# Attention blocks turned in pairs, with their high-half products moved behind their own turns

## The chip, the cores and the metric

One core of a Trainium2 chip runs the whole kernel in one launch. The metric is the time of one execution on the device, in microseconds; the kernel before was run three times (1393.4 to 1393.8 us, median 1393.6).

## The reference

One layer of a decoder on 1024 tokens of width 1024: RMSNorm and one wide input projection; two mixers beside each other, a sparse attention and a causal pooling; each is multiplied by a sigmoid gate (1024 channels each), added, projected and added to the residual; then RMSNorm, an MLP with squared ReLU (4096 wide), and a last RMSNorm. The attention has 8 heads of 64 in two groups of four, and three branches that each have a softmax of their own:

```
s_c = q k_cmp  - slope * dist        63 compressed keys
s_s = q k_slc  - slope * dist        all earlier keys (the 16 best of 16 blocks of 64)
s_w = q k_win  - slope * dist        the last 512 keys
o   = g0 * softmax(s_c) v_cmp + g1 * softmax(s_s) v_slc + g2 * softmax(s_w) v_win
```

Everything is float32.

## The kernel before, in words

Float32 products are made of rounded halves: x = hi + lo, and a product is three matmuls, `ahi*whi`, `alo*whi`, `ahi*wlo` (lines 2248 to 2250 in the helper `three`), each 128x512. The program is written out for each engine, with semaphores by hand; nothing is scheduled by a tool.

The attention stage, the one that is changed, has 16 iterations `it`, eight for each group of four heads, in the order of query tiles 7, 1, 6, 2, 5, 3, 4, 0 (`ITER`). A tile i has i+1 blocks of 128 keys of the selected branch (`slc`), up to five of the window (`win`), and one of the compressed keys (`cmp`, always last): 14, 5, 13, 7, 12, 9, 11 and 3 blocks. Block numbers B run on over all iterations. An iteration has four quarters r; `chunk(it, r)` is the list of blocks of a quarter, a quarter of the iteration's blocks, rounded.

For one block:

- `turn` (TensorE, line 2517): four 128x128 transposes, one per head, from the probabilities `prob` into bank B % 2 of `psX`. It waits for `pt_lo` of block B-2 (the bank is free).
- `prob_hi` (ACT, line 1215): rounds the bank to `pth[B % 2]`, 128x512. It waits for the turn and for the high product of B-2.
- `prob_lo` (DVE, line 1868): what the rounding left, to `ptl[B % 2]`. It waits for `prob_hi` and for the low product of B-2.
- `high_product` (TensorE, line 2532, `pth` times the values, waits `pt_hi`) and `low_product` (line 2538, `ptl`, waits `pt_lo`). Both add into bank 2 of `psX`. The `cmp` block has one product, of line 2545, which with the last low product forms `last_products`, at the end of the iteration or, in front of even iterations, a little into the next.

At the head of each quarter TensorE makes the scores of the next iteration for head r (lines 2495 to 2508). DVE adds the masks and takes the maxima (lines 1823, 1834, 1838) and makes the bias `nb` (line 1842); ACT takes three exponentials for them (line 1207, one per branch, the first waits for `nb`); DVE divides (lines 1854, 1856) and raises `p_ready`.

ACT has one queue in program order. In a quarter it holds: `prob_hi` of the first block, exponential 1, `prob_hi` of the second, exponential 2, and so on; in the first quarter of even iterations two `prob_hi` stand in front of exponential 1. This order is the same before and after.

In the first 14 iterations (`Z_STEPS`) the gate products of the mixers are spread between the block work: 16 steps per iteration, four per quarter, each step one k of a 1024-deep product, that is three matmuls (`gates(q, lo, hi)`, written into bank 2 or 3 of `psX`). `GATE_LEAD` puts two of the four steps of the first quarter of even iterations ahead of the first turn. `share` cuts what is left of a quarter's steps into 2 parts per block. The order within a quarter of n blocks was, for each block: its turn, the low product of the block two back, a part of the gate steps, the high product of the block one back, another part.

Of the kernel before, what the change touches and what calls it, by code (L numbers as in the profile page):

```python
# [16 lines left out]
def hybrid_trunk(nc, x, norm1_g, w_in, cmp_pe, cmp_w1, cmp_w2, w_attn_proj, w_pool, pool_scale,  # L17
# [75 lines left out]
    with ctx:  # L93
# [14 lines left out]
        def place(name, shape, dt=f32):  # L108
            off = cursor[0]
            cursor[0] += size_of(shape)  # L110
            assert cursor[0] <= END, (name, cursor[0] - END)
            return nc.alloc_sbuf_tensor_at(name, shape, dt, offset=off)
# [10 lines left out]
        gates = place("gates", [P, TT, HEADS, 3])  # L123
# [285 lines left out]
        def chunk(it, r):  # L409

            b = blocks(ITER[it][1])
            lo, hi = [round(len(b) * c / GR) for c in (r, r + 1)]
            return [(first_block[it] + k, *b[k]) for k in range(lo, hi)]
# [9 lines left out]
        Z_STEPS = 2 * KT - 2  # L423
# [3 lines left out]
        def gate_share(it, r):  # L427

            if it < Z_STEPS:
                return it + 1, KT // 2 * r, KT // 2 * (r + 1)  # L430
            c, n = (2 * r, 2) if it == Z_STEPS else (2 * GR + r, 1)
            return Z_STEPS + 1, c, c + n
# [6 lines left out]
        def prob_col(i, kind, kb):  # L439
            if kind == "slc":  # L440
                return kb * P
            if kind == "win":
                return n_slc(i) + (kb - (i + 1 - n_win(i) // P)) * P
            return n_slc(i) + n_win(i)
# [3 lines left out]
        def gate_bank(q, h):  # L448

            return psX[:, 2 if q == 0 and h == 1 else 3]  # L450
# [124 lines left out]
        block = ctx.enter_context(nc.Block())  # L575
# [1669 lines left out]
        def _(pe):  # L2245
            def three(ps, slot, k, w, hi, lo, cols, start, stop):

                nc.tensor.matmul(ps, whi[:, slot, w], hi[:, k, cols], start=start, stop=False)  # L2248
                nc.tensor.matmul(ps, whi[:, slot, w], lo[:, k, cols], start=False, stop=False)  # L2249
                return nc.tensor.matmul(ps, wlo[:, slot, w], hi[:, k, cols], start=False, stop=stop)  # L2250
# [233 lines left out]
            def scores(it, r):  # L2484
                g, i = ITER[it]
                e = it * GR + r
                s = it % 2
                if r == 0:
                    pe.wait_ge(q_lo, it + 1)
                if e >= 1:  # L2490
                    pe.wait_ge(m_slc, e)
                a, w = n_slc(i), n_win(i)
                for c in range(0, a, HALF):
                    n = min(HALF, a - c)
                    nc.tensor.matmul(psS0[:, c:c + n], qh[:, s, r], kS[:, g, c:c + n], start=True, stop=False)
                    last = nc.tensor.matmul(psS0[:, c:c + n], ql[:, s, r], kS[:, g, c:c + n], start=False, stop=True)  # L2496
                last.then_inc(s_slc, 1)
                if e >= 1:
                    pe.wait_ge(m_win, e)
                nt = w // P  # L2500
                whole = nt if nt == HALF // P else nt - 1
                if whole:
                    out, ks = psS1[:, 0:whole * P], kW[:, g, i + 1 - nt:i + 1 - nt + whole, 0:P]
                    nc.tensor.matmul(out, qh[:, s, r], ks, start=True, stop=False)
                    nc.tensor.matmul(out, ql[:, s, r], ks, start=False, stop=True)
                out, ks = psS1[:, whole * P:w + CP], kW[:, g, i, (whole - nt + 1) * P:WC]
                nc.tensor.matmul(out, qh[:, s, r], ks, start=True, stop=False)
                nc.tensor.matmul(out, ql[:, s, r], ks, start=False, stop=True).then_inc(s_win, 1)

            def turn(it, B, kind, kb):  # L2510

                g, i = ITER[it]
                if B >= 2:
                    pe.wait_ge(pt_lo, B - 1)
                col = prob_col(i, kind, kb)
                for r in range(GR):
                    last = nc.tensor.transpose(psX[:, B % 2, r * P:(r + 1) * P], PB[it % 2][:, r, col:col + P], ident[:])  # L2517
                last.then_inc(t_done, 1)

            def stacked(it, kind, kb):  # L2520

                return {"slc": vS, "win": vW}[kind][:, kb, ITER[it][0]]

            def high_product(it, B, kind, kb):

                if B == first_block[it]:
                    if it:
                        pe.wait_ge(o_ready, it)
                    else:
                        pe.wait_ge(z_ready, 2)  # L2530
                pe.wait_ge(pt_hi, B + 1)
                nc.tensor.matmul(psX[:, 2], stacked(it, kind, kb), pth[:, B % 2], start=B == first_block[it],
                                 stop=False).then_inc(high_done, 1)

            def low_product(it, B, kind, kb):

                pe.wait_ge(pt_lo, B + 1)
                nc.tensor.matmul(psX[:, 2], stacked(it, kind, kb), ptl[:, B % 2], start=False, stop=False).then_inc(low_done, 1)

            def last_products(it):  # L2540

                B = first_block[it + 1] - 1
                low_product(it, B - 1, *blocks(ITER[it][1])[-2])
                pe.wait_ge(pt_lo, B + 1)
                nc.tensor.matmul(psX[:, 2], vC[:, ITER[it][0]], pth[:, B % 2], start=False, stop=True).then_inc(high_done, 1)

            def gates(q, lo, hi):

                n, slot = NZ + q, (NZ + q) % 2
                for h, k in [divmod(c, KT) for c in range(lo, hi)]:  # L2550
                    if h == 0 and k == 0:
                        pe.wait_ge(w_lo, n + 1)
                    if k == 0 and q:
                        pe.wait_ge(z_ready, 2 * q + h if q > 1 or h else 1)
                    last = three(gate_bank(q, h), slot, k, k, ahi, alo, slice(h * HALF, (h + 1) * HALF), k == 0, k == KT - 1)
                    if k == KT - 1:
                        last.then_inc(u_done, 1)
# [8 lines left out]
                scores(0, r)  # L2566
                gates(0, lo, hi)
            for it in range(NIT):
                recent = []
                for r in range(GR):  # L2570
                    if it + 1 < NIT:
                        scores(it + 1, r)
                    if r == 0 and it and GATE_LEAD[it]:
                        last_products(it - 1)
                    todo = chunk(it, r)
                    q, g0, g1 = gate_share(it, r)
                    if it == r == 0 or not todo:
                        lead = g1 - g0
                    else:
                        lead = GATE_LEAD[it] if r == 0 else 0  # L2580
                    share = [g0 + lead + (g1 - g0 - lead) * k // max(1, 2 * len(todo)) for k in range(2 * len(todo) + 1)]
                    gates(q, g0, g0 + lead)
                    if r == 0:
                        pe.wait_ge(p_ready, GR * (it + 1))
                    for k, (B, kind, kb) in enumerate(todo):
                        turn(it, B, kind, kb)
                        if len(recent) > 1:
                            low_product(it, *recent[-2])
                        gates(q, share[2 * k], share[2 * k + 1])
                        if recent:  # L2590
                            high_product(it, *recent[-1])
                        recent.append((B, kind, kb))
                        gates(q, share[2 * k + 1], share[2 * k + 2])
                if it + 1 == NIT or not GATE_LEAD[it + 1]:
                    last_products(it)
            gates(2 * KT - 1, KT + GR, 2 * KT)
# [282 lines left out]
```

## Time and profile before

| | |
|---|---|
| median of 3 runs | 1393.6 us |
| the profiled execution: device time | 1393.44 us |
| the profiled execution: span | 1391.7 us |
| TensorE busy in it | 1377.7 us |
| DVE, ACT, POOL busy | 1034.5, 736.8, 198.6 us |
| granted TensorE clock | 0.998 |
| attention stage (scores of iteration 0 to the last block product) | 190.8 to 571.3 us |
| in it: turns | 148 blocks, 592 transposes |

In a timeline row the first number is the start in us from the span's start, the second the length of what is merged into the row, then engine, line, operation, tiles, shapes, and how many instructions; in brackets the idle time of the engine before it and what ended it. PE is the matmul side of TensorE, PEld its weight loads. The records of matmuls overlap, since they are pipelined: the distance of two starts is what a matmul takes of the engine's time, not the record's length.

### The profile page before, as it was taken

What the parts mean: (1) busy time and instruction counts of PE and PEld (TensorE: products, weight loads), DVE (VectorE), ACT (ScalarE), POOL (GpSimd) and SP (SyncE); (2) the same over time, 40 slices, a digit from 0 to 9 for tenths busy, and PEclk for the clock granted to TensorE, in tenths of its full rate; (3) what the DMA queues carried; (4) which work ended last, traced back from release to release, by engine and by line L of the source; (5) the groups of instructions that cost most, each with busy time, mean ns of one, the idle gap of its engine ahead of it and who ended that gap; (6) DMA issues with size and microseconds to landing.
All of it is one profiled execution on the core that took longest, in us unless ns stands there. A gap on an engine that the chain in (4) does not pass through costs nothing.

```text
span 1391.7 us, 19091 instructions
## 1 busy us (share of the span) xinstructions
PE 1377.7 (99%) x6589; PEld 1140.6 (82%) x6589; DVE 1034.5 (74%) x2040; ACT 736.8 (53%) x1427; POOL 198.6 (14%) x199
## 2 busy tenths in 40 slices
PE   9999999999999999999999999999999999999997
PEld 7788788888888888788888888888888888888886
DVE  7986577888788888866568877778695968777664
ACT  6433246666666666622235655545454646555554
POOL 5132000101010100000230030211213030302100
PEclk9999999999999999999999999999999999999999
DMA  6446531222221121654222174654639191836553
GB/s 222 129 144 179 153 92 57 65 61 58 62 72 57 47 65 54 219 184 162 77 91 91 47 143 100 127 109 88 132 81 161 53 165 56 155 88 133 94 167 121
DMA packets 162109, 151.75 MB, mean 109 GB/s; under 512 B 12659, under 2 KB 125095, under 8 KB 162016
## 3 DMA queue, kind: packets, MB, share of 16 engines
q1 hardware_dynamic: 145888, 121.20, 28.7%
q0 software_dynamic: 16128, 29.37, 14.4%
q8 instruction: 51, 0.84, 0.2%
q14 instruction: 42, 0.34, 0.1%
HBM read 94.43 MB, written 56.10 MB: 108 GB/s over the span
## 4 chain that ended last, share of the span: by engine, by line
PE 95%; DVE 3%; ACT 1%; issue 1%; DVEq 0%; POOL 0%; POOLq 0%; ACTq 0%
PE psU L2248 5%; PE psU L2249 5%; PE psU L2250 5%; PE psX L2517 5%; PE psU L2695 4%; PE psU L2697 4%; PE psX L2248 4%; PE psU L2696 4%; PE psX L2249 4%; PE psX L2250 4%; PE psU L2732 4%; PE psU L2734 4%; PE psU L2733 4%; PE psX L2695 3%; PE psX L2697 3%; PE psX L2696 3%
## 5 line engine op out<-in xcount | busy, mean ns | idle before, releaser
L1024 POOL DMA_DIRECT2D residual_scratch<-csum x112 | 98.2, 911 | 482.1 <-DVE csum L2147 414.4
L1970 DVE TENSOR_TENSOR ring_lo<-raw,ring_hi 128x512 fp32r<-128x512 f32 x150 | 103.1, 687 | 64.9 <-ACT ring_hi L1327 64.9
L1327 ACT ACTIVATE ring_hi<-raw 128x512 fp32r<-128x512 f32 x150 | 92.8, 626 | 63.8 <-PE psU L2734 22.8
L1215 ACT ACTIVATE pth<-psX 128x512 fp32r<-128x512 f32 x148 | 87.4, 596 | 71.2 <-PE psX L2517 71.0
L1868 DVE TENSOR_TENSOR ptl<-psX,pth 128x512 fp32r<-128x512 f32 x132 | 90.4, 688 | 29.4 <-ACT pth L1215 28.7
L1207 ACT ACTIVATE prob<-prob,nb 128x640 f32<-128x640 f32 (+7 forms) x128 | 93.8, 733 | 31.9 <-DVE nb L1842 31.7
L2248 PE MATMUL psX<-ahi,whi 128*128 128x512 f32 x256 | 102.8, 401 | 0.1
L2249 PE MATMUL psX<-alo,whi 128*128 128x512 f32 x256 | 100.8, 394 | 0.0
L2250 PE MATMUL psX<-ahi,wlo 128*128 128x512 f32 x256 | 100.4, 392 | 0.0
L2517 PE MATMUL psX<-ident,prob 128*128 128x128 f32 x592 | 88.4, 274 | 1.4 <-DVE prob L1856 0.6
L2248 PE MATMUL psU<-ahi,whi 128*128 128x512 f32 x216 | 84.7, 392 | 0.0
L996 POOL TENSOR_TENSOR wlo<-wraw,whi 128x1024 fp32r<-128x1024 f32 x14 | 33.6, 2401 | 357.1 <-DVE prob L1856 357.1
L2249 PE MATMUL psU<-alo,whi 128*128 128x512 f32 x216 | 84.1, 389 | 0.0
L2250 PE MATMUL psU<-ahi,wlo 128*128 128x512 f32 x216 | 84.1, 389 | 0.0
L2517 PEld LDWEIGHTS psX<-ident,prob 128*128 128x128 f32 x592 | 68.5, 140 | 16.1 <-DVE ptl L1868 4.2
L1402 ACT ACTIVATE csum<-psU 128x512 f32<-128x512 f32 x84 | 49.5, 598 | 39.2 <-PE psU L2734 31.0
L1408 ACT ACTIVATE csum<-csum 128x512 f32<-128x512 f32 x64 | 40.5, 633 | 49.8 <-DVE csum L2104 49.8
L1823 DVE CUSTOM_DVE_ANT_0 prob<-psU,T 128x1024 f32<-128x1024 f32 (+7 forms) x64 | 48.1, 752 | 24.4 <-PE psU L2496 24.3
L1970 DVE TENSOR_TENSOR ring_lo<-t,ring_hi 128x512 fp32r<-128x512 f32 x60 | 41.2, 686 | 32.3 <-ACT ring_hi L1327 32.3
L1854 DVE TENSOR_SCALAR prob<-prob,rs 128x640 f32<-128x640 f32 (+7 forms) x128 | 57.5, 492 | 2.3
L2250 PEld LDWEIGHTS psX<-ahi,wlo 128*128 128x128 f32 x256 | 48.1, 188 | 11.1
L1327 ACT ACTIVATE ring_hi<-t 128x512 fp32r<-128x512 f32 x60 | 37.8, 630 | 35.7 <-DVE t L1983 23.6
(374 smaller groups left out, 3989.0 us busy)
## 6 DMA issues: line engine op xcount, KB each, us to landing
raw<-in_w_ff_dram SPq DMA_DIRECT2D x120, 256.0 KB, 4.4
residual_scratch<-csum POOLq DMA_DIRECT2D x112, 256.0 KB, 5.9
wraw<-in_w_in_dram SPq DMA_DIRECT2D x23, 512.0 KB, 4.1
gate_scratch<-zst SPq DMA_DIRECT2D x32, 256.0 KB, 2.8
mg<-gate_scratch SPq DMA_DIRECT2D x16, 512.0 KB, 3.4
proj_scratch<-stage SPq DMA_DIRECT2D x30, 256.0 KB, 2.2
xt<-in_x_dram SPq DMA_DIRECT2D x8, 512.0 KB, 6.9
duo_w<-in_w_in_dram SPq DMA_DIRECT2D x16, 256.0 KB, 4.2
```

The lines of the kernel that those rows point to most:

```text
L1024: pool.dma_start(resid[rows, cols], sums[b][e][:], accum_op=ALU.add).then_inc(added[b][e], 16)
L1207: nc.scalar.activation(cols, cols, ACT.Exp, scale=2.0 ** -(g * GR + r + 1), bias=nb[:, it % 2, r, b:b + 1], accum_out=esum[:, it % 2, r, b ...
L1327: nc.scalar.activation(weights_of(g)[0], raw_of(g), ACT.Copy).then_inc(w_hi, 1)
L1868: nc.vector.tensor_tensor(dst[part, B % 2], psX[part, B % 2], pth[part, B % 2].bitcast(f32), ALU.subtract).then_inc(pt_lo, 1)
L1970: nc.vector.tensor_tensor(lo, raw_of(g), hi.bitcast(f32), ALU.subtract).then_inc(w_lo, 1)
L2248: nc.tensor.matmul(ps, whi[:, slot, w], hi[:, k, cols], start=start, stop=False)
L2249: nc.tensor.matmul(ps, whi[:, slot, w], lo[:, k, cols], start=False, stop=False)
L2250: return nc.tensor.matmul(ps, wlo[:, slot, w], hi[:, k, cols], start=False, stop=stop)
L2517: last = nc.tensor.transpose(psX[:, B % 2, r * P:(r + 1) * P], PB[it % 2][:, r, col:col + P], ident[:])
L2695: nc.tensor.matmul(ps, hi[:, k], a, start=first and k == 0, stop=False, skip_group_check=more)
L2696: nc.tensor.matmul(ps, hi[:, k], b, start=False, stop=False, skip_group_check=more)
L2697: last = nc.tensor.matmul(ps, lo[:, k], a, start=False, stop=k == HK - 1, skip_group_check=more)
```

## The change

In the first 14 iterations the blocks of a quarter are taken two at a time (an odd last one alone): both are turned, then the low products of all blocks at least two behind the newest turned one follow directly, then parts of the gate steps and the high products of these same blocks: part, high of the first, part, high of the second, part. The last two iterations keep the order of before. No instruction is added or removed, and DVE, ACT, POOL and SP keep theirs and their order.

```diff
@@ the loop over iterations
-                recent = []
+                done, low_next, late = [], 0, None
@@ in a quarter, behind the wait for p_ready
-                    for k, (B, kind, kb) in enumerate(todo):
-                        turn(it, B, kind, kb)
-                        if len(recent) > 1:
-                            low_product(it, *recent[-2])
-                        gates(q, share[2 * k], share[2 * k + 1])
-                        if recent:
-                            high_product(it, *recent[-1])
-                        recent.append((B, kind, kb))
-                        gates(q, share[2 * k + 1], share[2 * k + 2])
+                    size = 2 if it < Z_STEPS else 1
+                    for k in range(0, len(todo), size):
+                        turned = todo[k:k + size]
+                        for block in turned:
+                            turn(it, *block)
+                        while low_next < len(done) and done[low_next][0] + 2 <= turned[-1][0]:
+                            low_product(it, *done[low_next])
+                            low_next += 1
+                        end = 2 * (k + len(turned))
+                        at = share[2 * k]
+                        if size == 1:
+                            at = share[2 * k + 1]
+                            gates(q, share[2 * k], at)
+                            if late:
+                                high_product(it, *late)
+                                done.append(late)
+                            late = turned[0]
+                        else:
+                            for c, block in enumerate(turned):
+                                upto = share[2 * k + 2 * len(turned) - (2 if len(turned) == 2 and c == 0 else 1)]
+                                gates(q, at, upto)
+                                at = upto
+                                if block[1] != "cmp":
+                                    high_product(it, *block)
+                                    done.append(block)
+                        gates(q, at, share[end])
```

Three places on TensorE's queue. In the rows L2517 is a turn's transposes, L2532 a high product, L2538 a low one, L2248 to L2250 a gate step, L2495 the start of the next scores, and brackets name the semaphores waited for.

The first quarter of iteration 2 (three blocks, two gate steps left), before:

```order
L2517 MATMUL psX<-ident,prob_73 128x128 [waits pt_lo,p_ready]
L2517 MATMUL psX<-ident,prob_73 128x128 x3
L2517 MATMUL psX<-ident,prob_73 128x128 [waits pt_lo]
L2517 MATMUL psX<-ident,prob_73 128x128 x3
L2248 MATMUL psX<-ahi,whi 128x512
L2249 MATMUL psX<-alo,whi 128x512
L2250 MATMUL psX<-ahi,wlo 128x512
L2532 MATMUL psX<-pth,vS 128x512 [waits pt_hi,o_ready]
L2517 MATMUL psX<-ident,prob_73 128x128 [waits pt_lo]
L2517 MATMUL psX<-ident,prob_73 128x128 x3
L2538 MATMUL psX<-ptl,vS 128x512 [waits pt_lo]
L2532 MATMUL psX<-pth,vS 128x512 [waits pt_hi]
```

and after:

```order
L2532 MATMUL psX<-pth,vS 128x512 [waits pt_hi,o_ready]
L2248 MATMUL psX<-ahi,whi 128x512
L2249 MATMUL psX<-alo,whi 128x512
L2250 MATMUL psX<-ahi,wlo 128x512
L2532 MATMUL psX<-pth,vS 128x512 [waits pt_hi]
L2517 MATMUL psX<-ident,prob_73 128x128 [waits pt_lo]
L2517 MATMUL psX<-ident,prob_73 128x128 x3
L2538 MATMUL psX<-ptl,vS 128x512 [waits pt_lo]
L2532 MATMUL psX<-pth,vS 128x512 [waits pt_hi]
```

Ahead of these rows the same eight transposes stand as before. The first high product now follows them without the gate step between, and the third block's high product, which stood in the next quarter, follows its own turn with one low product between.

The first quarter of iteration 3 (two blocks, four gate steps), after:

```order
L2517 MATMUL psX<-ident,prob_78 128x128 [waits pt_lo,p_ready]
L2517 MATMUL psX<-ident,prob_78 128x128 x3
L2517 MATMUL psX<-ident,prob_78 128x128 [waits pt_lo]
L2517 MATMUL psX<-ident,prob_78 128x128 x3
L2248 MATMUL psX<-ahi,whi 128x512 [waits z_ready,w_lo]
L2249 MATMUL psX<-alo,whi 128x512
L2250 MATMUL psX<-ahi,wlo 128x512
L2248 MATMUL psX<-ahi,whi 128x512
L2249 MATMUL psX<-alo,whi 128x512
L2250 MATMUL psX<-ahi,wlo 128x512
L2532 MATMUL psX<-pth,vS 128x512 [waits pt_hi,o_ready]
```

Before, two gate steps stood between the two turns. Behind these rows now stand a gate step, the second block's high product and the last gate step; before, that high product came in the next quarter.

The first quarter of iteration 0 (four blocks, no gate step between them), as one piece of the difference:

```order
-L2532 MATMUL psX<-pth,vS 128x512
-L2517 MATMUL psX<-ident,prob_73 128x128 x4
-L2538 MATMUL psX<-ptl,vS 128x512
-L2532 MATMUL psX<-pth,vS 128x512
-L2517 MATMUL psX<-ident,prob_73 128x128 x4
-L2538 MATMUL psX<-ptl,vS 128x512
-L2532 MATMUL psX<-pth,vS 128x512
+L2532 MATMUL psX<-pth,vS 128x512 x2
+L2517 MATMUL psX<-ident,prob_73 128x128 x8
+L2538 MATMUL psX<-ptl,vS 128x512 x2
+L2532 MATMUL psX<-pth,vS 128x512 x2
```

Where a turn and a high product alternated, two now stand together, and there is one high product more in the quarter.

## Rows read from the trace of the kernel before

**Rows 1.** The page: span, busy time of each engine, granted clock in slices.

```profile
span 1391.7 us, 19091 instructions
...
PE 1377.7 (99%) x6589; PEld 1140.6 (82%) x6589; DVE 1034.5 (74%) x2040; ACT 736.8 (53%) x1427; POOL 198.6 (14%) x199
...
PEclk9999999999999999999999999999999999999999
```

**Rows 2.** The page: the chain that ended last, by engine.

```profile
PE 95%; DVE 3%; ACT 1%; issue 1%; DVEq 0%; POOL 0%; POOLq 0%; ACTq 0%
```

**Rows 3.** Attention stage by stretches: us, PE, PEld, DVE, ACT, POOL, clock, DMA.

```profile
192.00:382.00 190.00, 188.91 (x1028) 158.49 (x1027) 152.69 (x475) 125.06 (x302) 16.81 (x7) 1.00 0.21 59
382.00:572.00 190.00, 188.05 (x1025) 156.75 (x1025) 155.51 (x472) 128.48 (x308) 16.80 (x7) 1.00 0.23 69
```

**Rows 4.** The waits of PE, whole program: total us, times, longest.

```profile
PE psX L2532 <- ACT pth L1215: 1.0, 3, 0.3
...
PE psX L2545 <- DVE pth L1868: 0.6, 2, 0.3
PE psX L2517 <- DVE ptl L1868: 0.5, 3, 0.2
```

**Rows 5.** Timeline of PE, one turn and what follows it.

```profile
302.02 0.60 PE L2517 MATMUL psX<-ident,prob 128*128 128x128 f32 x4
302.37 0.48 PE L2538 MATMUL psX<-ptl,vW 128*128 128x512 f32 x1
302.69 0.39 PE L2248 MATMUL psX<-ahi,whi 128*128 128x512 f32 x1
302.92 0.40 PE L2249 MATMUL psX<-alo,whi 128*128 128x512 f32 x1
```

**Rows 6.** Timeline, first quarter of iteration 0.

```profile
210.30 1.06 PE L2517 MATMUL psX<-ident,prob 128*128 128x128 f32 x8
210.97 1.09 ACT L1215 ACTIVATE pth<-psX 128x512 fp32r<-128x512 f32 x2 [1.17 <-PE psX L2517]
211.71 0.47 PE L2532 MATMUL psX<-pth,vS 128*128 128x512 f32 x1 [0.34 <-ACT pth L1215]
...
213.62 0.42 PEld L2517 LDWEIGHTS psX<-ident,prob 128*128 128x128 f32 x4 [0.59 <-DVE ptl L1868]
...
214.50 0.58 ACT L1215 ACTIVATE pth<-psX 128x512 fp32r<-128x512 f32 x1
...
214.57 0.28 PE L2495 MATMUL psU<-kS,qh 128*128 128x256 f32 x1
```

**Rows 7.** Timeline, first quarter of iteration 2.

```profile
258.35 1.03 PE L2517 MATMUL psX<-ident,prob 128*128 128x128 f32 x8
...
259.14 0.48 PE L2248 MATMUL psX<-ahi,whi 128*128 128x512 f32 x1
...
259.92 0.39 PE L2532 MATMUL psX<-pth,vS 128*128 128x512 f32 x1
...
260.37 0.66 PE L2517 MATMUL psX<-ident,prob 128*128 128x128 f32 x4
...
260.96 0.17 DVE L1842 TENSOR_SCALAR nb<-mx 128x3 f32<-128x3 f32 x1
...
261.16 0.62 ACT L1207 ACTIVATE prob<-prob,nb 128x384 f32<-128x384 f32 x1 [1.09 <-DVE nb L1842]
...
261.78 0.58 ACT L1215 ACTIVATE pth<-psX 128x512 fp32r<-128x512 f32 x1
```

**Rows 8.** Timeline, first quarter of iteration 3.

```profile
283.53 0.60 PE L2517 MATMUL psX<-ident,prob 128*128 128x128 f32 x4
...
285.68 0.94 ACT L1207 ACTIVATE prob<-prob,nb 128x768 f32<-128x768 f32 x1 [0.66 <-DVE nb L1842]
...
286.62 0.58 ACT L1215 ACTIVATE pth<-psX 128x512 fp32r<-128x512 f32 x1
```

**Rows 9.** Timeline, the last product of iteration 0.

```profile
234.62 0.50 PE L2545 MATMUL psX<-pth,vC 128*128 128x512 f32 x1 [0.28 <-DVE pth L1868]
```

## Prediction

> **What bounds the kernel now.** I read the page's busy times first: TensorE is busy 1377.7 of 1391.7 us, at full granted clock, the next engine (DVE) 1034.5 [rows 1]. The chain that ended last agrees: 95% of it is TensorE [rows 2]. The change touches the attention stage alone, so the stretch view comes next: from 192 to 572 us TensorE is busy 377.0 of 380, but DVE is busy 81% and ACT 67% of it [rows 3]. So the time is the sum of what TensorE issues plus its waits; there is little left to gain in waits, and the two other engines have not much slack to lose. The list of TensorE's waits says who ends them: ACT's `pth` and DVE's `ptl` and `pth`, a handful of them [rows 4]. Timelines then give the price of each wait.
>
> **The sum.** No work is added or removed; only TensorE's queue is reordered. Two kinds of term are left: the cost of alternating between turns and products, and waits. The profiled execution took 1393.4 us (0.2 under the median); the sum is made on it.
>
> *Alternation.* A 128x512 product takes 0.23 us from start to start (302.69 to 302.92), but the first product behind a turn 0.32 (302.37 to 302.69) [rows 5]. That 0.09 looks like a switch cost to be halved. It isn't: the product starts 0.35 behind the turn's first transpose [rows 5], and 0.79 behind the first of eight [rows 7]. The second four thus take 0.44, and one turn with the product's extra 0.09 is 0.35 + 0.09 = 0.44 too: the 0.09 is the end of the last transpose. From such differences a switch is worth 0.01 us at most. The change makes 50 pairs, 7 of which already stood as eight transposes in a row (first quarters of the even iterations); 43 x 0.01 = **-0.4**.
>
> *Waits.* What matters is the distance from a turn to its own high product. Before, another turn and as a rule gate steps lay between; now only the partner's turn, the low products behind, and the quarter's gate steps up to it. `pt_hi` needs the turn's end, 0.05 to ACT, 0.6 of conversion, 0.05 back; and whatever ACT's unchanged queue holds in front.
>
> (a) First quarters of iterations 2, 4, 6, 10, 12: the first high product stands directly behind eight transposes. Rows 6 show that very sequence: it starts 1.41 us behind the first transpose where rows 7 show an unhindered product at 0.79. Of the 0.62, 0.03 is the longer record of the turns (1.06 against 1.03): 0.59 each, 5 x 0.59 = **+2.95**.
>
> (b) In the same places a wait goes. The third turn started 0.45 behind the high product (259.92 to 260.37) instead of 0.23, and its record is 0.06 longer than an unhindered one (0.66 against 0.60) [rows 5, 7]: it waited for `ptl` of the first block, which is early enough now. 5 x 0.28 = **-1.4**.
>
> (c) The same five quarters' third block is alone, and its high product follows its own turn and one low product. By hand for iteration 2: turns at 258.35, first high 259.73, gate step, second high 260.65, turn 260.88, low 261.24, high possible at 261.56. But ACT has exponential 1 in front of this block's conversion; it waits for `nb` (260.96 + 0.17), starts at 261.16, and the conversion starts at 261.78 and ends at 262.36 [rows 7]. None of these moves forward, since `nb` comes from DVE's masks. High at 262.41: a wait of 0.85. Iteration 10 is the same. In 4 and 12 the exponential is 512 wide instead of 384; by (0.94 - 0.62)/3 [rows 7, 8] that is 0.11 more on ACT and, I take it, as much again in DVE's masks: 1.07. In 6 it is short, and the floor stays: 0.60 + 0.05 + 0.58 + 0.05 = 1.28 behind the turn's start against 0.36 + 0.32: 0.6. Sum 2 x 0.85 + 2 x 1.07 + 0.6 = **+4.4**. Bounds: 0.3 each (ACT idle and half the floor) and 1.1 each.
>
> (d) First quarters of 0 and 8, four blocks, no gate step between. In iteration 0 the fourth turn starts at 213.62, held by DVE's `ptl` [rows 6], and doesn't move. Before, the scores came at 214.57 [rows 6], so the last high product at 214.34. Now: low 213.98, low 214.30, high 214.53, and the fourth block's high when ACT's conversion ends, 214.50 + 0.58 + 0.05 = 215.13; scores at 215.36. Of the 0.79 later, 0.23 is a product taken over from the next quarter: 0.56. In iteration 8 I expect the same or somewhat more, 0.74. **+1.3**.
>
> (e) Last product of 0 and 8: it waits already, 0.28 idle and 0.16 by which a record (0.39) is longer than a product's 0.23 [rows 9]. The chain it waits for (turn, ACT, DVE) now starts behind the partner's turn, while TensorE's work up to it is the same. Between 0 and 0.7, taken 0.45 each: **+0.9**.
>
> (f) First quarters of 3, 5, 11, 13, two blocks. Iteration 3 by hand: turns 283.53, gate steps from 284.32, first high 285.79, gate step, second high possible at 286.71. ACT's exponential (768 wide) holds the second conversion until 286.62; it ends at 287.20 [rows 8]: wait 0.53. The 640 wide ones of 5 and 13: 0.11 less on ACT. 2 x 0.53 + 2 x 0.42 = **+1.9**.
>
> (g) All other pairs have four gate steps in the quarter. In three-block quarters two steps lie before the second high, enough; in four-block ones (eight pairs in 0, 2, 8, 10) the second high comes 2.35 behind the turn, ACT with one exponential between is done at 2.5 or so: 8 x 0.15 = **+1.1** with rounding. Bounds 0 and 2.5.
>
> Sum: -0.4 + 2.95 - 1.4 + 4.4 + 1.3 + 0.9 + 1.9 + 1.1 = +10.75, or 1404.2. Behind the stage TensorE goes on without a wait of size, so nothing gives it back.
>
> The turns run at 109 ns per transpose (0.44 / 4), in fours and eights alike, and the granted clock of the stage is 1.00 [rows 3], which is the 2.4 GHz level. The Trainium skill ("TensorE: Matmul & The Clock Gate", Part 4) speaks against grouping: it says that transposes do not count as activity for the clock gate. By that rule longer runs of turns could bring the lower level; the trace has eight in a row and no fall.
>
> **The rivals.**
>
> *The clock falls* (by that rule, as a mechanism here): pairs of turns, with a wait behind, bring the 1.2 GHz level. If just the 50 pairs took twice their 0.88 us, it would be 44 us: 1448. Against it: eight transposes with a wait of 0.6 behind leave the clock at 1.00 [rows 3, 6]. Chance 0.02.
>
> *Faster: the alternation does cost.* If the 0.09 behind each turn [rows 5] is a price of switching and conversions come in time, 43 x 0.09 = 3.9 goes, and (b) 1.4: 1388.1. It decides if (a) to (g) stay under 5.3 us. For it: nothing but the 0.32; against it the eight transposes of rows 7, and the wait of rows 6, which shows (a) as it will be. Chance 0.03.
>
> *No change: waits only move.* Highs done earlier let ACT and DVE run earlier, and they shorten later waits by what they cost. It would need ACT to be early at the next quarter; but TensorE, once late, isn't caught up by anyone, since every wait of it is time on the chain. 1392 to 1395. Chance 0.05.
>
> *Much slower: DVE joins the chain.* Pairs ask for conversions in bursts of two, each burst 2 x (0.6 + 0.7) us of ACT and DVE against some 3.2 us of TensorE's work; with DVE at 81% a late burst delays masks, exponentials and the next burst. If each of the 50 pairs waited 0.4 us: +20, 1413. For it: rows 3; against: the first turn of a pair needs only `ptl` of the first block before. Chance 0.10.
>
> **How the numbers follow.** My forecast, 1404.2, has the remaining 0.80. Its low end is (c) at 0.3 each, (f) at 0.2, (d) at 0.4, (e) and (g) at 0: -0.4 + 2.95 - 1.4 + 1.5 + 0.8 + 0.8 = +4.3, 1397.7. Its high end is (c) at 1.1, (e) at 0.7, (f) at 0.65, (g) at 2.5, (d) at 0.9: -0.4 + 2.95 - 1.4 + 5.5 + 1.8 + 1.4 + 2.6 + 2.5 = +15, 1408.4. 1397.7 to 1409 leaves out the rivals and some of the ends, about 2 in 10. A measurement of this kernel tells 0.2%, 2.8 us, from no change. Faster by more: 0.03; within: 0.05; slower: 0.92 (forecast, clock, DVE).
>
> **What would show it.** In the profile after, TensorE's waits for ACT `pth` at line 2532 should grow from 3 to some thirty, with about 10 us in starts that come late; in the first quarter of iteration 2 the first high starts 1.4 us behind the first transpose, the third 1.5 behind its turn. The turns' wait for `ptl` in those quarters is gone. The span of the stage grows by what the time does, DVE's and ACT's busy times stay. I am wrong if the high products start without idle time (then ACT's conversions were earlier than I follow here), if the first product behind eight transposes takes 0.23, or if the stretch behind the attention changes its length.

## The result and the profile after

The change makes the kernel slower: 1407.3 us (median of 6 runs, 1406.9 to 1407.6) against 1393.6, ratio 1.0096, interval 1.0086 to 1.0106. The forecast was 1404.2 in a range of 1397.7 to 1409.0. The profiled execution took 1407.1 us with a span of 1405.4, 13.7 more than before; this section accounts for these 13.7.

The page of the changed kernel, which answers to [rows 1, 2]:

```profile
span 1405.4 us, 19091 instructions
...
PE 1382.8 (98%) x6589; PEld 1140.2 (81%) x6589; DVE 1036.1 (74%) x2040; ACT 731.4 (52%) x1427; POOL 198.8 (14%) x199
...
PEclk9999999999999999999999999999999999999999
...
PE 90%; DVE 6%; ACT 2%; issue 1%; DVEq 0%; POOL 0%; ACTq 0%; POOLq 0%
```

The same instructions, the same granted clock, and 8% of the chain now runs over DVE and ACT where it was 4%. By stretches, to be read beside [rows 3]:

```profile
192.00:382.00 190.00, 184.66 (x992) 152.68 (x991) 147.52 (x458) 119.15 (x294) 16.83 (x7) 1.00 0.20 58
382.00:572.00 190.00, 184.86 (x994) 152.82 (x993) 150.92 (x459) 120.47 (x294) 16.84 (x7) 1.00 0.19 56
```

TensorE issues 67 instructions fewer in the same 380 us (1986 against 2053), and DVE and ACT are less busy in them too: no engine has become the bound by its load, each waits for another. From the last block product to the end of the program it is 820.4 us before and 820.5 after (571.3 to 1391.7, 584.9 to 1405.4), so the whole loss is in the attention stage and nothing is given back. The list of TensorE's waits, for [rows 4]:

```profile
PE psX L2532 <- ACT pth L1215: 7.9, 18, 0.9
...
PE psX L2545 <- DVE pth L1868: 1.3, 2, 0.7
PE psX L2517 <- DVE ptl L1868: 0.7, 2, 0.6
```

The high products' waits for ACT grew from 3 to 18. The view counts idle time alone. The record of an unhindered product is 0.39 us long, while the next one starts 0.23 behind it, so the record's end covers 0.16 us of a wait and the view shows less than the starts are late.

The first quarter of iteration 2, which answers to [rows 7]:

```profile
260.60 1.09 ACT L1215 ACTIVATE pth<-psX 128x512 fp32r<-128x512 f32 x2 [0.35 <-PE psX L2517]
...
261.34 0.47 PE L2532 MATMUL psX<-pth,vS 128*128 128x512 f32 x1 [0.34 <-ACT pth L1215]
261.65 0.39 PE L2248 MATMUL psX<-ahi,whi 128*128 128x512 f32 x1
...
262.35 0.40 PE L2532 MATMUL psX<-pth,vS 128*128 128x512 f32 x1
...
262.58 0.17 DVE L1842 TENSOR_SCALAR nb<-mx 128x3 f32<-128x3 f32 x1
262.59 0.60 PE L2517 MATMUL psX<-ident,prob 128*128 128x128 f32 x4
...
262.78 0.61 ACT L1207 ACTIVATE prob<-prob,nb 128x384 f32<-128x384 f32 x1 [1.09 <-DVE nb L1842]
262.94 0.47 PE L2538 MATMUL psX<-ptl,vS 128*128 128x512 f32 x1
...
263.39 0.57 ACT L1215 ACTIVATE pth<-psX 128x512 fp32r<-128x512 f32 x1
...
264.02 0.50 PE L2532 MATMUL psX<-pth,vS 128*128 128x512 f32 x1 [0.61 <-ACT pth L1215]
264.36 0.40 PE L2248 MATMUL psX<-ahi,whi 128*128 128x512 f32 x1
```

Terms (a) to (c) stand here one behind the other. The first high product starts (261.34) when ACT's first conversion has ended, with idle time before it. The third turn starts at 262.59, 0.24 behind the second high product: no wait for `ptl` any more. The low product starts at 262.94, the high one could at 263.26 and starts at 264.02, 0.76 late. The chain view of this stretch says why:

```profile
260.60 0.61 ACT pth L1215
...
261.23 0.69 DVE ptl L1868
261.93 0.46 DVE prob L1834
262.40 0.14 DVE kC L1838
262.58 0.18 DVE nb L1842
...
263.30 0.19 ACT prob L1207
263.49 0.49 ACT pth L1215
...
264.02 0.50 PE psX L2532
```

From the first block's conversion it goes to DVE (its `ptl`, then the masks of the next iteration, then `nb`), back to ACT (exponential, then the third block's conversion) and to the product. TensorE's own turn of the third block isn't in the chain: it was done at 263.19. Nor is the first high product with its 0.59 us of waiting: by this chain the third one would start at 264.02 with or without that wait.

Iteration 3's second high product, for [rows 8]:

```profile
288.99 0.94 ACT L1207 ACTIVATE prob<-prob,nb 128x768 f32<-128x768 f32 x1 [0.68 <-DVE nb L1842]
...
289.92 0.57 ACT L1215 ACTIVATE pth<-psX 128x512 fp32r<-128x512 f32 x1
...
290.55 0.50 PE L2532 MATMUL psX<-pth,vS 128*128 128x512 f32 x1 [0.40 <-ACT pth L1215]
```

And the last product of iteration 0, for [rows 9], with what follows it:

```profile
235.77 0.50 PE L2545 MATMUL psX<-pth,vC 128*128 128x512 f32 x1 [0.64 <-DVE pth L1868]
...
236.10 0.39 PE L2495 MATMUL psU<-kS,qh 128*128 128x512 f32 x1
```

**Where the 13.7 us are.** I compared the starts of the scores that head each quarter in both traces. A quarter that takes a high product over from the next shows 0.23 too much, and the last quarter of an iteration 0.23 too little; with that taken out:

| term | forecast | measured |
|---|---|---|
| (a), (b), (c): first quarters of 2, 4, 6, 10, 12 | +5.95 | 7.67 - 5 x 0.23 = +6.5 |
| (d): first quarters of 0, 8 | +1.3 | 2.26 - 0.46 = +1.8 |
| (e), and (g) in the same places: last quarters of 0, 8 | +0.9 + 0.6 | 0.79 + 0.46 = +1.25 |
| (f): first quarters of 3, 5, 11, 13 | +1.9 | 3.40 - 4 x 0.23 = +2.5 |
| the rest of (g), and alternation: everything else | +0.5 - 0.4 | +1.65 |
| sum | +10.75 | +13.7 |

The last quarters of 0 and 8 have four blocks each, so half of (g) lies in them. The last product's idle time grew there from 0.28 to 0.64 and 0.66: 0.7 us for (e), and 0.5 is left for (g). Of the last row, 0.8 lies in the third quarters of iterations 2 and 10 (0.39 each), and 0.8 in iterations 1 and 9, whose quarters hold a single block or two. What remains is +0.07, so the -0.4 of the alternation is not to be seen.

The split between (a) and (c) is one of order only: in iterations 2, 4, 10 and 12 the third block's high product is held by the chain above, and without (a) it would have waited 0.59 longer.

### The profile page after: what moved, and what is told of

It reads as the page before. It is cut to its first block, busy times and chain, and to the rows that moved or that the text cites. A ratio compares the mean times of both kernels' runs of the same rounds, so it can differ in the third digit from the quotient of the medians.

```text
span 1405.4 us, 19091 instructions
## 1 busy us (share of the span) xinstructions
PE 1382.8 (98%) x6589; PEld 1140.2 (81%) x6589; DVE 1036.1 (74%) x2040; ACT 731.4 (52%) x1427; POOL 198.8 (14%) x199
## 4 chain that ended last, share of the span: by engine, by line
PE 90%; DVE 6%; ACT 2%; issue 1%; DVEq 0%; POOL 0%; ACTq 0%; POOLq 0%
PE psU L2248 5%; PE psU L2249 5%; PE psU L2250 5%; PE psU L2712 4%; PE psU L2714 4%; PE psU L2713 4%; PE psX L2517 4%; PE psU L2749 4%; PE psU L2751 4%; PE psU L2750 4%; PE psX L2248 4%; PE psX L2249 4%; PE psX L2250 3%; PE psX L2712 3%; PE psX L2714 3%; PE psX L2713 3%
## 5 line engine op out<-in xcount | busy, mean ns | idle before, releaser
L2248 PE MATMUL psX<-ahi,whi 128*128 128x512 f32 x256 | 102.2, 399 | 0.3 <-ACT zst L1229 0.2
L2250 PE MATMUL psX<-ahi,wlo 128*128 128x512 f32 x256 | 100.3, 392 | 0.0
L2248 PE MATMUL psU<-ahi,whi 128*128 128x512 f32 x216 | 84.7, 392 | 0.0
L2250 PE MATMUL psU<-ahi,wlo 128*128 128x512 f32 x216 | 84.1, 389 | 0.0
L2517 PE MATMUL psX<-ident,prob 128*128 128x128 f32 x592 | 81.9, 274 | 1.4 <-DVE ptl L1868 0.7
L2517 PEld LDWEIGHTS psX<-ident,prob 128*128 128x128 f32 x592 | 66.4, 140 | 9.0 <-DVE ptl L1868 1.8
L2250 PEld LDWEIGHTS psX<-ahi,wlo 128*128 128x128 f32 x256 | 48.1, 188 | 11.2
```

## The experiments

Two theories. **Distance**: a high product waits because it stands too near its own turn; its conversion is ready 1.3 us behind the turn's start, and later where ACT's queue holds an exponential in front. **Burst**, the rival: turning in pairs hands ACT and DVE two conversions at a time, and that costs wherever pairs stand, however the high products lie. Kernels sent together share the runs of the kernel before (medians 1393.4 and 1393.9).

### Pairs in the later quarters only, and in the first quarters only

```diff
# e1_later
-                    size = 2 if it < Z_STEPS else 1
+                    size = 2 if it < Z_STEPS and r > 0 else 1
...
+                        if size == 2 and late:
+                            high_product(it, *late)
+                            done.append(late)
+                            late = None
# e2_first
-                    size = 2 if it < Z_STEPS else 1
+                    size = 2 if it < Z_STEPS and r == 0 else 1
```

> The pairs are made in the second to fourth quarters only; first quarters keep the order of before (a high product left over is issued behind the next pair's turns). Distance theory (a high product waits because it stands too near its own turn, above all in first quarters, where ACT's queue holds an exponential in front and few gate steps lie between): the first quarters cost 10.8 of the 13.7 us of the change, so about 3 us are left, 1396.6 (1395.5 to 1398). Burst theory (two conversions at a time load ACT and DVE, wherever the pairs stand): 34 of the 50 pairs are left and the loss goes with them, 9 us, 1402.6.

> The other half: pairs in the first quarters of the first 14 iterations only, the order of before in the other quarters. Distance theory: the 10.8 us of the first quarters, 1404.4 (1403.5 to 1405.5). Burst theory: 16 of 50 pairs, 4.4 us, 1398.

Measured: 1396.6 (ratio 1.0023, interval 1.0013 to 1.0033) and 1403.7 (1.0074, 1.0057 to 1.0091). Counted from the lists of blocks, 13 of the 50 pairs stand in first quarters and 37 in the later ones (the expectations say 16 and 34). The 37 bring 3.2 us and the 13 bring 10.2, three quarters of the loss; together that is the change's 13.7 within 0.3. By numbers of pairs alone it would have been 10.1 and 3.6. It is the place of a pair that counts, not the number. Of the 13, 7 already stood as eight transposes, and there the change regrouped no turns. In the second kernel's list of waits:

```profile
PE psX L2532 <- ACT pth L1215: 7.2, 16, 0.8
```

and in the first one's:

```profile
PE psX L2545 <- DVE pth L1868: 1.3, 2, 0.7
...
PE psX L2532 <- ACT pth L1215: 1.0, 3, 0.3
```

With pairs in later quarters alone, the high products have as little idle time in front as before; what is left is (e), the last product, and waits too short to leave idle time in this view.

### All pairs, the high products one block behind

The second block's high product moves behind the next pair's turns; the first block's stays behind its own pair.

```diff
+                        if size == 2 and late:
+                            high_product(it, *late)
+                            done.append(late)
+                            late = None
...
-                                if block[1] != "cmp":
+                                if c + 1 == len(turned) and block[1] != "cmp":
+                                    late = block
+                                elif block[1] != "cmp":
                                     high_product(it, *block)
```

> All pairs stay, but the second block's high product (and a lone block's) is issued behind the turns of the next pair, as before the change; the first block's stays behind its own pair. Distance theory: the waits of the third block in even iterations (4.7 us with the slower restart behind them) and of the second block in iterations 3, 5, 11, 13 (2.5) go; those of the first block behind eight transposes stay (5 x 0.6 and 0.1 more each for the restart), and the second turn of a pair in a four-block quarter waits for ptl by up to 0.6 in iterations 0, 2, 8, 10: about 5 us over before, 1398.6 (1397.5 to 1400). Burst theory: turns come two at a time as in the change, so nearly all of the 13.7 us stay, 1405 or more.

Measured: 1398.3 (1.0035, 1.0022 to 1.0047). All 50 pairs stand and 9 of the 13.7 us are gone, as the distance theory had it and against the burst theory. What is left changed its kind:

```profile
PE psX L2517 <- DVE ptl L1868: 2.8, 8, 0.6
PE psX L2532 <- ACT pth L1215: 2.7, 8, 0.3
```

The first line is the second turn of a pair, which waits for its bank: here the pairs do cost something of their own, 2.8 us of idle time. That is a fifth of the change's loss, but more than half of the 4.9 us left in this kernel; in the changed kernel the same line shows 0.7.

### No pairs, each high product behind its own turn

```diff
-                    size = 2 if it < Z_STEPS else 1
+                    own = it < Z_STEPS
+                    size = 1
...
-                        if size == 1:
+                        if not own:
```

> No pairs: the blocks are turned one at a time as before the change, but each high product follows its own turn (with the quarter's gate steps in between as share gives them), in the first 14 iterations. Distance theory: without the partner's turn and the second low product in between, nearly every high product of the 120 waits for its conversion, by 0.2 to 0.9 us, and each wait costs 0.1 more for the restart: about 43 us over before, 1436 (1430 to 1444; without a restart cost 1430). Burst theory (the pairs are what costs): no pairs, no loss, 1393 to 1396.

Measured: 1436.8 (1.0311, 1.0295 to 1.0327).

```profile
PE psX L2532 <- ACT pth L1215: 27.2, 55, 0.8
```

Without a single pair the loss is three times that of the change, 43 us, which the burst theory can't give. The two halves of the change thus pull against each other: high products behind their own turns cost, and pairing softens it, since the partner's turn (0.44) and a second low product (0.23) give the conversion 0.7 us of cover.

### ACT's queue

```diff
-                    early = 1 if r == 0 and it % 2 == 0 and len(todo) > 1 else 0
-                    if early:
-                        prob_hi(todo[0][0], todo[0][1])
+                    early = min(len(todo) - 1, 2) if r == 0 else 0
+                    for b in todo[:early]:
+                        prob_hi(b[0], b[1])
```

> TensorE's order is that of the change; on ACT, in first quarters, up to three conversions stand in front of the first exponential (both of two blocks, three of three). Distance theory with ACT's queue: the waits of iterations 3, 5, 11 and 13 go whole (2.5 us), those of the third block fall from 0.77 and 1.02 to the bare conversion, 0.6 (2 x 0.15 + 2 x 0.4), iteration 0 gains 0.2: 4 us less than the change, 1403.4 (1402.5 to 1404.5). If the queue on ACT is not what holds them (DVE, or the turn itself), the time stays at 1407.3; if later exponentials then delay the next iteration, it is above.

Measured: 1403.2 (1.0069, 1.0052 to 1.0086), 4.1 less than the change. In iteration 3 the two conversions now stand together and the second high product has no wait:

```profile
288.44 1.08 ACT L1215 ACTIVATE pth<-psX 128x512 fp32r<-128x512 f32 x2
...
289.74 0.94 ACT L1207 ACTIVATE prob<-prob,nb 128x768 f32<-128x768 f32 x1 [0.23 <-DVE nb L1842]
```

By quarters, the first ones of 3, 5, 11 and 13 fall by 0.62 to 0.69 each and are back at the kernel before; those of 2, 4, 10 and 12 fall by 0.16 to 0.41, and in all of them the third high product starts 1.28 to 1.30 us behind its own turn, the floor of (c); one quarter of iteration 1 grows by 0.46. So all of (f) and all of what (c) had over its floor, 3.8 us of the 13.7, needed the exponential in front, and the rest of the loss stays with this queue too.

### A gate step between the turns and the first high product

In the changed kernel, both gate steps of the even iterations' first quarters move. In quarters of three blocks one goes from behind the first high product to its front, the other from behind the third high product to its front:

```diff
+                    if r == 0 and 0 < it < Z_STEPS and it % 2 == 0:
+                        share = [g0 + lead + min(g1 - g0 - lead, c) for c in (0, 0, 1, 1, 1, 2, 2, 2, 2)]
```

> The change, with the two gate steps of even iterations' first quarters put elsewhere: one between the eight transposes and the first high product, the other behind the second. Distance theory: a step is 0.69 us, so the 0.59 waits of the first high product (6 places, with 0.1 of restart each) go; the third block's wait falls a little in 2, 4, 10, 12 and by 0.6 in 6; iteration 8 loses some at its fourth turn. About 4.6 us less than the change, 1402.7 (1401.5 to 1404). If these waits were only moved on to the next wait, the time stays near 1407.

Measured: 1402.9 (1.0067, 1.0051 to 1.0082), 4.4 less than the change. The time came as expected, but not by the wait that the expectation names. Iteration 2:

```profile
260.23 1.04 PE L2517 MATMUL psX<-ident,prob 128*128 128x128 f32 x8
261.02 0.48 PE L2248 MATMUL psX<-ahi,whi 128*128 128x512 f32 x1
...
263.48 0.40 PE L2250 MATMUL psX<-ahi,wlo 128*128 128x512 f32 x1
264.29 0.50 PE L2532 MATMUL psX<-pth,vS 128*128 128x512 f32 x1 [0.41 <-ACT pth L1215]
264.63 0.34 PE L2495 MATMUL psU<-kS,qh 128*128 128x384 f32 x1
```

The first high product's wait is gone, yet the third starts 4.06 us behind the first transpose (260.23 to 264.29), as in the changed kernel (4.05). In 4, 10 and 12 it is the same (4.29, 4.05 and 4.29 in both): there the wait only moved on to the third high product, which the chain through `nb` holds. The quarter is 0.7 shorter because the second gate step no longer stands behind that product but inside its wait. In iteration 6, where the exponential is short, the third high product starts 0.32 earlier as well, and the quarter is 1.0 shorter; in 8 it is 0.68. No run moves the first step alone; by these starts it would win nothing in 2, 4, 10 and 12.

### What an alternation costs

In the kernel before, the low product moves into the middle of the turn, so that there are 116 alternations more:

```diff
                 for r in range(GR):
+                    if r == 2 and between is not None:
+                        low_product(it, *between)
                     last = nc.tensor.transpose(
```

> The kernel before, with each low product moved from behind a turn to its middle (two transposes, low product, two transposes), 116 times: one alternation between transposes and products more in each block. By the difference of starts read before the prediction (0.01 us a switch at most) it costs 0.8, and the turn's later end 1.1 in waits for the last products: 1395.5 (1394.5 to 1396.5). If the first product behind transposes really paid 0.09 for the switch, it costs 10 us more: 1405.

Measured: 1395.4 (1.0013, 1.0003 to 1.0022). Its timeline:

```profile
303.03 0.38 PE L2519 MATMUL psX<-ident,prob 128*128 128x128 f32 x2
303.16 0.48 PE L2540 MATMUL psX<-ptl,vW 128*128 128x512 f32 x1
303.49 0.38 PE L2519 MATMUL psX<-ident,prob 128*128 128x128 f32 x2
303.62 0.48 PE L2248 MATMUL psX<-ahi,whi 128*128 128x512 f32 x1
303.94 0.40 PE L2249 MATMUL psX<-alo,whi 128*128 128x512 f32 x1
```

Turn, low product and gate product take 0.91 (303.03 to 303.94), where they took 0.90 with one alternation fewer (302.02 to 302.69 and one product of 0.23) [rows 5]. The product behind a pair of transposes shows 0.33 and 0.32, but the transposes in front show correspondingly less. Grouping turns has next to nothing to gain in this kernel.

### Gate steps moved in the kernel before

The same lever without the change: the order of the blocks is that of before, and the two gate steps are placed around the first high product.

```diff
+                    if r == 0 and 0 < it <= Z_STEPS and it % 2 == 0:
+                        share = [g0 + lead + min(g1 - g0 - lead, c) for c in (0, 0, 0, 1, 2, 2, 2, 2, 2)]
```

> The kernel before, its order of blocks, with gate steps of the first quarters of even iterations (2 to 14) moved only: one in front of the first high product, one directly behind it. The waits of the third turn (0.28 each in 2, 4, 6, 10, 12) go, in 8 and 14 the 0.59 waits of the first high product; two waits of 0.27 come at the next quarter's first turn. About 2.1 us less than before: 1391.4 (1390.8 to 1392.2), which would beat both kernels. If TensorE's waits were hidden by something else, no change.

Measured: 1391.7 (0.9985, 0.9976 to 0.9994), 2.2 us less than before and the fastest of all. The place of (b), in its timeline:

```profile
260.11 0.40 PE L2532 MATMUL psX<-pth,vS 128*128 128x512 f32 x1
260.34 0.39 PE L2248 MATMUL psX<-ahi,whi 128*128 128x512 f32 x1
...
261.03 0.60 PE L2517 MATMUL psX<-ident,prob 128*128 128x128 f32 x4
```

The third turn now has a gate step in front instead of 0.28 us of waiting. By quarters, 1.3 of the 2.2 us come from iterations 8 and 14, where the first high product had stood directly behind eight transposes before as well. The gain is small, and its interval reaches close to no change.

## Why the prediction was right

- **What bounds the kernel** held: TensorE issues almost without a break, and the 820.4 us behind the stage did not change. That every wait of it is time did not hold: in iterations 2, 4, 10 and 12 the chain over DVE and ACT fixes the third high product, and a wait in front of it costs nothing of its own.
- **Alternation** at 0.01 us or less held, by the timeline of the split turns. The rival that rested on 0.09 was wrong by mechanism: by it the split turns would have cost 10 us, and they cost 1.6.
- **(a)** held: the first high product started 1.38 behind the first transpose in all five places, 0.59 late, as read from iteration 0 before. Only with (c) does it make a sum, though; by itself it would be worth its 0.59 in iteration 6 alone.
- **(b)** held: the waits for `ptl` are gone there.
- **(c)** held in mechanism and in its chain through `nb`, which the chain view shows link by link. By hand 0.85, 1.07 and 0.6; 0.76, 1.01 and 0.61 were measured, each with 0.11 more on the start behind it.
- **(d), (f)** held in mechanism and were 0.5 and 0.6 short; of (d), iteration 8 took 1.15 where 0.74 was expected. **(e)** came at 0.7 for 0.9, **(g)** at 1.3 for 1.1. Iterations 1 and 9, which the working put at nothing, took 0.8.
- **DVE joining the chain** by late bursts, and pairs as the cause, fell with the kernel whose high products lag. DVE is on the chain all the same, through `nb`, as (c) had it. **Waits that only move** fell as a forecast for the change with 1407.3 itself; as a mechanism it is real, and the moved gate steps show it in four quarters.
- **The clock** stayed at 1.00 in the stage, the 2.4 GHz level, with 50 pairs of turns in it, some of them with a wait behind. The Trainium skill's statement ("TensorE: Matmul & The Clock Gate", Part 4) that transposes do not count as activity did not bring the lower level here.

The sum was 3 us short, and one thing it left out explains most: **a wait costs more than its length**. At 264.02 the product that had waited starts, and the next one 0.34 behind it, not 0.23. The same stands in rows of the trace before that I had not used: 234.62 the last product of iteration 0, 234.96 the scores. In the trace after there are 22 such places (20 high products and the last products of 0 and 8), 0.11 each, and the five of (a), where the product behind comes 0.31 behind (261.34 to 261.65), 0.08 too many: 2.7 us, against 0.3 in the trace before, so 2.4 of the 3. In the kernel without pairs, 58 places of the same kind hold 6.1 us. The expectations of the experiments had this cost in, and came within 0.8 us each; for that kernel they gave 1436 with it and 1430 without, and 1436.8 was measured, though its range was wide (1430 to 1444). The 0.6 that is left is the difference of terms too low (iterations 1 and 9 above all) and too high ((c), (e)). That 1407.3 lies in the range is partly luck: the high end, 1408.4, had no restart in it, and held because it left room for a (g) of 2.5 that measured 1.3. The count of waits was too high (some thirty named, 18 in the view), since the short ones leave no idle time between the records.

## What to carry to other kernels

When a product consumes what another engine makes of an earlier step, count the distance in the bounding engine's own work, and compare it with the whole way of the data, including what the converting engine's queue holds in front: here 1.3 us at best, and 3.3 in iteration 3, where an exponential that itself waits for DVE stands between (second turn at 287.25, its product at 290.55). Work that needs nothing (here gate steps) belongs exactly into that distance, in front of the product that the longest chain holds; moving two such steps of 0.7 us in each of six quarters won 4.4 us, while regrouping turns won nothing in any run. A shorter wait in front of such a product is no gain. Grouping like instructions is worth trying only if the difference of starts, not the single longer record behind a group, shows a price for alternating.

## What the runs showed of the hardware

TensorE's restart: a product held by a semaphore starts together with its own weight load (at most 0.03 us behind it), and the next product comes 0.11 us late, 0.08 behind eight transposes. The weight loads of the changed kernel at the place above:

```profile
264.02 0.19 PEld L2532 LDWEIGHTS psX<-pth,vS 128*128 128x128 f32 x1 [0.92 <-ACT pth L1215]
264.13 0.19 PEld L2248 LDWEIGHTS psX<-ahi,whi 128*128 128x128 f32 x1
264.36 0.19 PEld L2249 LDWEIGHTS psX<-alo,whi 128*128 128x128 f32 x1
```

In an unhindered row each load runs beside the product before it. Here the weights (`vS`, ready long before; only the moving `pth` was late) were loaded at 264.02, when the wait was over, and the next load began 0.11 later. The Trainium skill ("TensorE: Matmul & The Clock Gate", the table of figures at its head) says that the queue pulls weight loads ahead of matmuls in flight. The trace agrees for unhindered stretches, but in none of the 25 waits of the stage that left idle time in front of a high product, a last product or a turn did its load start more than 0.03 us ahead of it. In the program the wait stands in front of load and product both, so the trace doesn't tell whether a load could pass a wait that held the product alone.
